# The Fourier half's GpSimd copy ahead of the second norm's steps, and the router product in four groups of 32 columns

## What is computed

```python
h = rmsnorm(x, norm1_g) * (1 + mod[:, 1]) + mod[:, 0]
a, states = mixer(h, ...)          # 4 mLSTM heads (512 columns) and a Fourier half (512), then @ w_out
x = x + mod[:, 2] * a
h = rmsnorm(x, norm2_g) * (1 + mod[:, 4]) + mod[:, 3]
x = x + mod[:, 5] * expert_choice_moe(h, ...)
```

```python
aff = jax.nn.softmax((xf @ router_w).astype(jnp.float32), axis=-1)   # router_w: 1024 x 16
gate, idx = lax.top_k(aff.T, cap)                                    # each expert picks its tokens
```

## Time and profile before

| | |
|---|---|
| median of 3 runs | 2329.23 us (2328.97 to 2329.26) |
| the profiled execution | 2327.72 us |
| its span, first to last instruction | 2325.9 us |
| TensorE busy | 2183.0 us, 94% |
| VectorE, ScalarE, GpSimd busy | 487.9, 350.6, 270.3 us |
| mean granted TensorE clock | 0.973 of full speed |
| `mixing` in the trace | about 420 to 723 us, its turns from about 460 |

### The profile page before, as it was taken

One profiled execution on the slowest core, in us unless ns is written; L12 is line 12 of the kernel. 1 busy time (PEld: TensorE's weight loads), 2 busy tenths in 40 slices (PEclk: granted clock), 3 DMA queues, 4 the chain that ended last, 5 costly groups with the idle time before them and its releaser, 6 DMA issues. The chain is left out here.

```text
span 2325.9 us, 36974 instructions
## 1 busy us (share of the span) xinstructions
PE 2183.0 (94%) x15013; PEld 1887.1 (81%) x15013; DVE 487.9 (21%) x1246; ACT 350.6 (15%) x995; POOL 270.3 (12%) x266
## 2 busy tenths in 40 slices
PE   7999999999983699999999999999999999999992
PEld 2445554775541699999999999999999999999992
DVE  1111115457657101111110011101011111001102
ACT  1011112132320011111101111111011111111102
POOL 0000000202120102102012021020220211202102
PEclk9999999999996799999999999999999999999996
DMA  9720100644316559798697797976978969769765
GB/s 376 303 100 32 63 32 36 220 152 143 131 64 202 179 172 362 218 319 273 240 363 217 268 333 223 350 236 245 363 216 299 296 234 365 217 248 356 220 248 182
DMA packets 351602, 528.76 MB, mean 227 GB/s; under 512 B 12997, under 2 KB 292285, under 8 KB 348233
## 3 DMA queue, kind: packets, MB, share of 16 engines
q1 hardware_dynamic: 336456, 509.35, 63.2%
q0 software_dynamic: 15104, 18.88, 3.9%
HBM read 492.23 MB, written 35.95 MB: 227 GB/s over the span
## 5 line engine op out<-in xcount | busy, mean ns | idle before, releaser
L1652 PE MATMUL ps_ab<-xeT,ring 128*128 128x144 f32 x8192 | 1008.5, 286 | 14.7 <-DVE xeT L1697 14.7
L1652 PEld LDWEIGHTS ps_ab<-xeT,ring 128*128 128x128 f32 x8192 | 1006.9, 190 | 14.8 <-issue 14.8
L1665 PE MATMUL ps_yy<-hidT,ring 128*128 128x144 f32 x4096 | 504.4, 286 | 0.0
L1665 PEld LDWEIGHTS ps_yy<-hidT,ring 128*128 128x128 f32 x4096 | 502.8, 190 | 0.0
L464 PE MATMUL ps_p<-w_in_sb,hT 128*128 128x512 f32 x720 | 318.1, 595 | 3.0 <-DMA w_in_sb<-in_w_in 3.0
L1701 DVE TENSOR_TENSOR hidT<-silu,ps_ab 128x144 f32<-128x144 f32 x256 | 77.9, 304 | 886.4 <-ACT silu L1619 823.5
L464 PEld LDWEIGHTS ps_p<-w_in_sb,hT 128*128 128x128 f32 x720 | 134.6, 191 | 156.6 <-issue 155.5
L1598 POOL DMA_INDIRECT stream<-ye,slot_row x64 | 100.9, 1577 | 1215.9 <-DVE ye_p L1712 1201.3
L1619 ACT ACTIVATE silu<-ps_ab 128x144 f32<-128x144 f32 x256 | 74.4, 290 | 909.3 <-PE ps_ab L1652 875.1
L1137 PE MATMUL b_z<-y,shared 128*128 128x512 f32 x288 | 127.9, 597 | 15.1 <-issue 6.5
L1137 PEld LDWEIGHTS b_z<-y,shared 128*128 128x128 f32 x288 | 53.2, 190 | 79.4 <-issue 76.4
(11 more groups left out here) (259 smaller groups left out, 1060.5 us busy)
## 6 DMA issues: line engine op xcount, KB each, us to landing
ring<-in_exp_w SPq DMA_DIRECT2D x384, 1024.0 KB, 12.4
y<-in_ada_w SPq DMA_DIRECT2D x22, 1024.0 KB, 8.0
w_in_sb<-in_w_in SPq DMA_DIRECT2D x4, 2048.0 KB, 21.5
shared<-kvo SPq DMA_DIRECT2D x15, 512.0 KB, 6.1
kvo<-pr SPq DMA_DIRECT2D x9, 768.0 KB, 3.3
qkT_dram<-qkT SPq DMA_DIRECT2D x9, 512.0 KB, 4.9
qk<-qkT_dram SPq DMA_DIRECT2D x9, 512.0 KB, 5.2
m_in<-m_lanes SPq DMA_DIRECT2D x9, 512.0 KB, 5.9
```

Source lines behind the costliest of these rows:

```text
L1652: mm = nc.tensor.matmul(ps_ab[f % 2][:, N * w:N * w + N], unit[:, k, bass.ts(c, P)], xeT[:, k], start=(k == 0), stop=(k == DT - 1))
L1665: mm = nc.tensor.matmul(ps_yy[d % 2][:, 0:N], unit[:, f % 2, bass.ts(d, P)], hT[:, f], start=(f == 0), stop=(f == FT - 1))
```

## The change

GpSimd's copy L951 moves from behind L944 to directly behind L934 of the same turn, with its waits. The router tile has 32 columns in each of its eight blocks, of which the last 16 are zero. Product k of the eight goes to the partitions 32j to 32j + 31 of the bank, with j = k mod 4, so that each of four column groups accumulates two products. The logit copy takes all 128 partitions, and the turned result has four partial logits for each token; VectorE adds them in an extra reduction to a tile `logit_rows` in SBUF, from which the maximum and the exponential are then taken. At the block's start the memset of the logit tile is replaced by one of the router tile, and SP waits for it before the router's load.

```diff
--- before.py
+++ after.py
@@ -777,7 +777,8 @@
         n_init, n_out = sb("n_init", [LANES, HD]), g.end_n
         c_end = sb("c_end", [P, LANES, VW])
         carry = g.carry
-        router = sb("router", [P, DT, E])
+        router = sb("router", [P, DT, 2 * E])
+        logit_rows = sb("logit_rows", [P, E])
         logits = g.gate_rows[:, 0:P]
         aff = sb("aff", [P, E])
         soft = sb("soft", [P, 4])
@@ -789,7 +790,7 @@
         b_n = [bank(f"b_n{i}") for i in range(2)]
         b_i = [bank(f"b_i{i}") for i in range(2)]
         b_z = [bank(f"b_z{i}") for i in range(2)]
-        ps_logits, ps_affT = b_z[1][0:E, 0:P], b_s[0:E, 0:P]
+        ps_logits, ps_affT = b_z[1][:, 0:P], b_s[0:E, 0:P]
         sem = g.sem
         pair = lambda name: [sem(f"{name}{i}") for i in range(2)]
         qk_loaded, m_loaded, v_loaded = g.front_loaded[0:2], g.front_loaded[2:4], g.front_loaded[4:6]
@@ -803,7 +804,7 @@
         end_turned, end_kept = sem("end_turned"), sem("end_kept")
         states_stored = g.states_stored
         o_loaded, xr_loaded, stream_stored = pair("o_loaded"), pair("xr_loaded"), pair("stream_stored")
-        normed_stored, consts_loaded, ones_set = sem("normed_stored"), sem("consts_loaded"), sem("ones_set")
+        normed_stored, consts_loaded, buffers_set = sem("normed_stored"), sem("consts_loaded"), sem("buffers_set")
         (scores_summed, x_ready, w_ready, p_ready, inter_summed, inter_kept, intra_summed, comb_done,
          out_summed, out_kept, x2_ready, sq_summed, rms2_ready, xn2_ready, x2_turned, h2T_dve, h2T_act,
          logits_summed, logits_kept, logits_turned, negmax_ready, soft_exped, aff_ready, aff_turned, aff_kept,
@@ -874,7 +875,8 @@
                 load(1, 1, True)
                 with nc.allow_non_contiguous_dma("head gains, one per partition"):
                     sp.dma_start(head_g[:], g.head_g.rearrange("a (h v) -> v (a h)", v=HD)).then_inc(consts_loaded, 16)
-                sp.dma_start(router[:], g.router_w.rearrange("(k p) e -> p k e", p=P)).then_inc(consts_loaded, 16)
+                sp.wait_ge(buffers_set, 1)
+                sp.dma_start(router[:, :, 0:E], g.router_w.rearrange("(k p) e -> p k e", p=P)).then_inc(consts_loaded, 16)
                 for n in range(KV, TILES - 1):
                     load_kv(n)
                 sp.wait_ge(end_kept, 3)
@@ -932,6 +934,13 @@
                     if on(i, 1):
                         pool.wait_ge(hms_ready, i)
                         nc.gpsimd.tensor_tensor(hms[:], hms[:], g.minus_half[:], ALU.pow).then_inc(rh_ready, 1)
+                    if on(i, 1):
+                        if below(i, 2):
+                            pool.wait_ge(f_kept, PAIRS // 2 + 1)
+                            pool.wait_ge(kv_summed, TILES - 1)
+                        elif not below(i, 3):
+                            pool.wait_ge(out_summed, 2 * i - 4)
+                        nc.gpsimd.tensor_copy(mixT[:, 1 - par, HEADS:DT], g.fuT[:, :, bass.ts(i - 1, P)]).then_inc(mix_pool, 1)
                     if on(i, 2):
 
                         pool.wait_ge(sq_summed, 2 * i - 2)
@@ -942,13 +951,6 @@
                         nc.gpsimd.tensor_tensor(ss[:, 2:3], ss[:, 2:3], g.eps[:], ALU.add).then_inc(ss_steps, 1)
                         pool.wait_ge(ss_steps, T * 2 + 2)
                         nc.gpsimd.tensor_tensor(ss[:, 3:4], ss[:, 2:3], g.minus_half[:, 0:1], ALU.pow).then_inc(rms2_ready, 1)
-                    if on(i, 1):
-                        if below(i, 2):
-                            pool.wait_ge(f_kept, PAIRS // 2 + 1)
-                            pool.wait_ge(kv_summed, TILES - 1)
-                        elif not below(i, 3):
-                            pool.wait_ge(out_summed, 2 * i - 4)
-                        nc.gpsimd.tensor_copy(mixT[:, 1 - par, HEADS:DT], g.fuT[:, :, bass.ts(i - 1, P)]).then_inc(mix_pool, 1)
                     if on(i, 2):
 
                         pool.wait_ge(rms2_ready, T + 1)
@@ -1027,7 +1029,7 @@
                         act.wait_ge(negmax_ready, i - 3)
                         if not below(i, 5):
                             act.wait_ge(aff_turned, i - 4)
-                        did(nc.scalar.activation(aff[:], b_z[1][:, 0:E], ACT.Exp, bias=soft[:, 0:1], accum_out=soft[:, 1:2]), soft_exped)
+                        did(nc.scalar.activation(aff[:], logit_rows[:], ACT.Exp, bias=soft[:, 0:1], accum_out=soft[:, 1:2]), soft_exped)
                     if on(i, 0):
                         inter(i, 0)
                     for p in fill[1:2]:
@@ -1190,10 +1192,11 @@
                     pe.wait_ge(h2T_dve, i - 3)
                     pe.wait_ge(h2T_act, i - 3)
                     for k in range(DT):
-                        mm = nc.tensor.matmul(ps_logits, router[:, k], h2T[:, k], start=(k == 0), stop=(k == DT - 1))
+                        j = k % 4
+                        mm = nc.tensor.matmul(ps_logits[32 * j:32 * j + 2 * E], router[:, k], h2T[:, k], start=(k < 4), stop=(k >= 4))
                     mm.then_inc(logits_summed, 1)
 
-                pe.wait_ge(ones_set, 1)
+                pe.wait_ge(buffers_set, 2)
                 z_sum(0)
                 pe.wait_ge(start_loaded, 32)
                 for d in range(2):
@@ -1275,10 +1278,10 @@
                 did, settle = g.dve.did, g.dve.settle
                 TT, TS, STT = nc.vector.tensor_tensor, nc.vector.tensor_scalar, nc.vector.scalar_tensor_tensor
                 COPY = nc.vector.tensor_copy
-                did(nc.vector.memset(logits[:], 0.0))
+                did(nc.vector.memset(router[:], 0.0), buffers_set)
                 did(nc.vector.memset(g.aff_rows[:], 0.0))
                 did(nc.vector.memset(g.eps[:], EPS))
-                did(nc.vector.memset(va[:, :, :, HD], 1.0), ones_set)
+                did(nc.vector.memset(va[:, :, :, HD], 1.0), buffers_set)
                 did(nc.vector.memset(g.states[:, 0], 0.0))
 
                 def weigh_kv(n):
@@ -1388,12 +1391,14 @@
                         dve.wait_ge(logits_summed, i - 3)
                         if not below(i, 5):
                             dve.wait_ge(logits_turned, i - 4)
-                        did(COPY(logits[0:E, :], ps_logits), logits_kept)
+                        did(COPY(logits[:], ps_logits), logits_kept)
                     if on(i, 1):
                         outputs(i, par, half)
                     if on(i, 4):
                         dve.wait_ge(logits_turned, i - 3)
-                        did(nc.vector.tensor_reduce(soft[:, 0:1], b_z[1][:, 0:E], AX.X, ALU.max, negate=True), negmax_ready)
+                        did(nc.vector.tensor_reduce(logit_rows[:], b_z[1][:, 0:P].rearrange("p (j e) -> p e j", j=4)[:, 0:E], AX.X, ALU.add))
+                        settle()
+                        did(nc.vector.tensor_reduce(soft[:, 0:1], logit_rows[:], AX.X, ALU.max, negate=True), negmax_ready)
                     if on(i, 3):
 
                         dve.wait_ge(rms2_ready, i - 2)
@@ -1430,7 +1435,7 @@
                         combine(i, 1)
 
                 turns(dve, g.dve, turn, {
-                    "dve_steps": 42, "x_ready": 4, "p_ready": 4, "negmax_ready": 2, "out_kept": 4, "x2_ready": 4,
+                    "dve_steps": 44, "x_ready": 4, "p_ready": 4, "negmax_ready": 2, "out_kept": 4, "x2_ready": 4,
                     "comb_done": 4, "aff_ready": 2, "xn2_ready": 2, "aff_kept": 2, "h2T_dve": 2, "hms_ready": 2, "hm_ready": 2,
                     "logits_kept": 2})
                 settle()
```

## The result

The changed kernel takes 2335.14 us (median of 8 runs, 2330.16 to 2337.47) where the kernel before takes 2329.1 (8 runs, 2328.24 to 2329.58): a ratio of 1.0022, 95% interval 1.0013 to 1.0031. It is slower by some 5 to 6 us, and its median lies outside the forecast range of 2323.0 to 2334.0. Its runs spread over 7 us where those of before spread over 1.3 beside them. The profiled execution took 2336.05 us with a span of 2334.2, 8.3 more than the span of before.

What follows compares the result with a forecast made beforehand. TensorE was taken as the bound, with the loop through head outputs and exponential setting the period in turns 4 to 8. Terms of -5.2 us plus +5.1 for clock falls gave -0.1: 2329.2 us, range 2323.0 to 2334.0.

Steps and rivals of the forecast that it cites:

- the clock's term: Second projection halves, turns 4 to 9: TensorE's clock falls behind three of six holes, 1.7 us each, +5.1 us.
- The clock falls in all six holes: Rival, turns 4 to 9: a fall behind every hole, -5.2 + 6 x 1.7 = +5.0, 2334.2 us; chance 0.13.
- Which loop sets the period: Turns 4 to 8: loop through head outputs and exponential sets the period; the 1.56 us hole is slack that moves later.
- The size of the hole: Ahead of the second projection half: idle time collects to 2.7 us in turns 4 to 8, 2.8 in turn 9.
- the router product's gain: TensorE's 16 router passes in four column groups: 1.2 us instead of 1.76, gain 0.56; bounds 0 and 1.1.
- the loop: Turned rows through head outputs and exponential to the second half: +0.25 us per turn, +1.25 over turns 4 to 8.
- the earlier normed rows: VectorE's L1357 and L1360 beside GpSimd's L958, which starts earlier: what comes after starts 0.36 us earlier.
- The price of a fall: Lowered clock on the second projection half: 6 x 0.28 = 1.7 us of full-speed work, from the stretch 496 to 502.
- Turns 11 and 12: No projection, router product at half clock: 2 x (0.30 - 1.33) = -2.06 us.
- Turn 9: No scores, VectorE's chain starts at the router's end but is held by L958: net -0.2 us.
- Sum without the clock: All terms of the mixing block without clock effects: -5.2 us; -1.6 with no overlap of the groups.
- The rival by the page: Turns 4 to 9: clock stays up, at most one fall, -5.2 to -3.5, 2324.0 to 2325.7 us; chance 0.22.

Runs made afterwards that it cites:

- the filled hole: Changed kernel plus three useless TensorE products between the intra products and the projection's second half, turns 4 to 8: 2321.89 us, ratio 0.9970.
- the part-filled hole: Changed kernel plus one useless TensorE product between the intra products and the projection's second half, turns 4 to 8: 2325.52 us, ratio 0.9982.
- the copy behind the output: Changed kernel with GpSimd's moved copy also waiting for VectorE's last head output: 2326.68 us, ratio 0.9991.
- the last version: Changed kernel with logits turned and summed early, copy behind the last head output, normed rows behind the second weighting: 2303.66 us, ratio 0.9891.
- the early logits: Changed kernel, logits turned mid first projection half, VectorE's sum and maximum ahead of the head outputs: 2307.73 us, ratio 0.9912.

## Why the prediction was wrong

The step that failed is the clock's term: "I take three of six, +5.1", with its price of 1.7 us. In the profiled execution the clock fell in five turns and took 133.4 - 121.6 = 11.8 us (turns 4 to 8 against those of the filled hole); between the medians of the two kernels it is 2335.14 - 2321.89 = 13.3. So by the medians the term was 8.2 us too small, and the other terms, -7.5 for the forecast -5.2, took 2.3 of that back. That is the distance from the forecast of -0.1 to the result of +6.0. The mechanism was the forecast's own. "The clock falls in all six holes", priced at 2334.2, came nearest, partly by luck: it was five falls and not six, three of them dearer than 1.7, and the other terms were off the other way.

- **Which loop sets the period.** Right, and shown: the hole left the place ahead of the first half, appeared ahead of the second, and turns 4 to 8 gained nothing from either part.
- **The size of the hole.** Forecast 2.7 us, measured 3.3 to 3.6. With the size that was forecast (the part-filled hole) the count of falls was two of five at 1.7 us, near the guess; behind the four holes of 3.5 us and more the clock fell each time. The fifth, of 3.26, could have gone either way by the table above. Two terms made the hole longer:
  - the router product's gain, 0.56 forecast and 1.27 measured. I let the two passes of one product follow each other at 0.11; they run four at a time, whether neighbouring products lie in different groups or in the same. My upper bound, 1.1, was too low as well. By the Trainium skill, "TensorEngine Tiling (Array Packing)", section "Theoretical Speedup", 32 columns give up to 4x; the 16 starts span 0.38 us and spanned 1.65 before, so here the page was right and my estimate from neighbouring rows was not. The drain on changing the mode, which the section "Key Properties" of the same page of the Trainium skill states, can't be told here: the step from the product ahead to the router's is 0.20 us in both kernels;
  - the loop, +0.25 forecast and +0.56 measured. The last head output (L1381, now L1384) was forecast 0.31 longer (0.32), the sum 0.26 (0.25), the exponential 0.04 (0.04). What was off is the earlier normed rows: 0.36 forecast, 0.05 measured. L960 now stands right behind the step that it waits for, and starts 0.16 us behind its end instead of 0.06 ahead, and VectorE's next small instruction came 0.15 us behind the release, not 0.04.
- **The price of a fall.** 1.7 us held in turns 4 and 5 and in every fall of the part-filled hole. In turns 6 to 8 it was 2.9: the clock went down about 1 us ahead of the second half and stayed at half about twice as long. The price came from one stretch, 496 to 502. The trace of before has a longer one that I did not price, at the start of the block: at half from 419 to 425, with TensorE busy from 420.87 on, where eight passes took 3.78 us that take 1.89 at full clock.

```profile
420.87 3.78 PE L1087 MATMUL b_z<-const,y 128*128 128x256 f32 x8 [1.79 <-DVE va L1281]
...
436.42 1.89 PE L1087 MATMUL b_z<-const,y 128*128 128x256 f32 x8
...
419.00:425.00 6.00, 4.21 (x12) 3.17 (x12) 1.94 (x6) 0.31 (x1) 0.00 (x0) 0.50 0.60 199
```

- **Turn 3** -2.20: exact (525.71 against 526.13, in an execution that was 1.78 late). **Turn 10** -2.06: -2.30. **Turns 11 and 12** -2.06: -0.49 - 1.28 = -1.77, near by luck. The first of the two products met the full clock and took 0.64 us instead of 3.35, but turn 11 gained only 0.49: VectorE's normed rows (L1407) ran beside GpSimd's L960, took 2.48 us instead of 0.74, and held back the affinities that TensorE turns next. **Turn 9** -0.2: -1.87, with the larger gain of the router, and its hole 1.42 us and without a fall where 2.8 and a chance of one were forecast.
- **Start of the block** +0.1: the wait for the memset grew from 1.79 to 1.93.
- **Sum without the clock** -5.2: the filled hole gives -5.6 between the profiled executions and -7.5 between the medians. The parts measured above sum to -5.4, with the errors of turn 9 and of the loop against each other.
- **The rival by the page.** By the Trainium skill, "TensorE: Matmul & The Clock Gate", section "Why this matters for your kernels", only idle gaps somewhat longer than the 2.7 us of the forecast are warned of. The runs speak against it as a limit: the clock fell behind single holes of 2.07 and 2.39 us, and outlasted four of 3.25 to 3.34. The longest holes of the changed kernel, 3.56 to 3.64, are of the size that it does warn of, and there the trace agrees: a fall behind each.

## What to carry to other kernels

When an engine waits in two places of a turn, ask which wait belongs to a loop through other engines. Taking the other away moves its idle time into the first; there it can be long enough to lower TensorE's clock, and then an edit that shortens TensorE's work makes the kernel slower. Break the loop first (here: the logits turned in the middle of the projection's first half instead of behind it), and the same edit is worth 18 us (2325.71 - 2307.73); where it can't be broken, even useless matmuls in the hole pay (2335.14 to 2321.89 us here).

## What was not expected of the hardware

- Sixteen passes of 128 moving columns in four column groups take 0.64 to 0.67 us in two different orders of the code, in one group 1.93.
- A lowered clock can cost 2.9 us of a 7.1 us run of matmuls, and repeat in every turn: the three turns with such a fall are 27.24, 27.28 and 27.28 us long. Holes of 2.95 to 3.34 us in turns of 24.1 had one fall in five.
- VectorE holds GpSimd as GpSimd holds VectorE: steps of 0.19, 0.19 and 0.56 us took 0.62, 0.52 and 1.01 beside VectorE's head outputs.
- A kernel with such holes has no sharp time. The runs of the changed kernel spread over 7.3 us and those with the copy behind the output over 12.6; with the hole filled it is 1.8, in the last version 0.6 (4 runs). But the early logits, with no such hole, spread over 4.3 in 4 runs, and the kernel before over 1.3 in the first comparison and 3.8 in the last, so holes in the turns are not the only cause. The 13 traces reach the first projection at 504.3 to 507.4 us, ahead of any such hole.
